# A mixture-of-experts layer on one Trainium2 core: one-hot rows shared out among three engines, gates interleaved in PSUM, and the gathered sum moved to VectorE

## The reference

```python
q = (h @ wq).reshape(B, S, PEER_HEADS, 2, PEER_QDIM // 2)
sub_scores = jnp.einsum('bshpk,hpnk->bshpn', q, subkeys)
top_v, top_i = lax.top_k(sub_scores, PEER_TOPK)
cand = top_v[..., 0, :, None] + top_v[..., 1, None, :]
cand_i = top_i[..., 0, :, None] * N_KEYS + top_i[..., 1, None, :]
best_v, best_pos = lax.top_k(cand.reshape(..., 256), PEER_TOPK)
expert = jnp.take_along_axis(cand_i.reshape(..., 256), best_pos, axis=-1)
gates = jax.nn.softmax(best_v, axis=-1)
hid = gelu(jnp.einsum('tkd,td->tk', u[expert], x), approximate=False) * gates
out = jnp.einsum('tk,tkd->td', hid, v[expert])
```

## Time and profile before

| what | value |
|---|---|
| median of 3 runs | 3908.99 us (3905.73 to 3910.11) |
| profiled execution | 3904.9 us |
| its span, first to last instruction | 3903.1 us |
| mean granted PE clock | 0.921 of full speed |
| busy, share of the span | PE 89%, PEld 72%, DVE 56%, ACT 37%, POOL 21% |
| gates, about 594 to 1012 us; dense, about 1012 to 1942 us | 418 us and 930 us |

### The profile page before, as it was taken

The page is one execution under the profiler, slowest core; times in us unless marked ns, Lnnn a source line. Parts: engine busy times, 40 slices in busy tenths (PEclk is TensorE's granted clock), DMA queues, the critical chain, the costliest instruction groups (busy, mean ns, idle before and its releaser), DMA issues.

```text
span 3903.1 us, 40841 instructions
## 1 busy us (share of the span) xinstructions
PE 3473.6 (89%) x16313; PEld 2806.0 (72%) x16313; DVE 2200.8 (56%) x3309; ACT 1446.3 (37%) x2342; POOL 830.0 (21%) x654
## 2 busy tenths in 40 slices
PE   5897998887799999999999997899898899899998
PEld 3466577777688888888878885678776574477887
DVE  2445597776588888888855524545532332344332
ACT  1222124665455555555532224444441111223222
POOL 0000102776355555555400000000000000000000
PEclk9895998989999999999989998899997598799999
DMA  4330522444888888888545522121121032022222
GB/s 170 130 114 1 195 75 102 168 161 147 303 302 293 306 298 294 305 298 293 205 130 184 186 95 81 68 84 69 59 92 37 1 97 86 6 97 82 97 97 76
DMA packets 189678, 574.02 MB, mean 147 GB/s; under 512 B 16368, under 2 KB 80496, under 8 KB 171056
## 3 DMA queue, kind: packets, MB, share of 16 engines
q1 hardware_dynamic: 152160, 369.80, 27.5%
q0 software_dynamic: 37328, 201.61, 14.3%
HBM read 523.69 MB, written 47.64 MB: 146 GB/s over the span
## 4 chain that ended last, share of the span: by engine, by line
PE 54%; DVE 32%; ACT 9%; issue 3%; DMA 2%; POOL 0%; SPq 0%; DVEq 0%; ACTq 0%; POOLq 0%
PE ps L228 10%; PE ps L230 10%; PE ps L229 10%; DVE peer_TG L1486 5%; PE ps L237 5%; DVE Wl L220 4%; DVE peerv_UV L1477 4%; DVE peerv_VL L1362 4%; DVE peerv_HI L1486 3%; ACT Wh L214 3%; PE ps L312 2%; PE ps L168 1%; ACT peerv_VH L1358 1%; ACT peerg_GB L1281 1%; DVE peerg_OH L1227 1%
## 5 line engine op out<-in xcount | busy, mean ns | idle before, releaser
L220 DVE TENSOR_TENSOR Wl<-W,Wh 128x1024 fp32r<-128x1024 f32 x363 | 438.7, 1209 | 778.8 <-ACT Wh L214 778.7
L214 ACT ACTIVATE Wh<-W 128x1024 fp32r<-128x1024 f32 x363 | 377.1, 1039 | 590.6 <-PE ps L230 569.5
L1409 POOL TENSOR_TENSOR peer_Y<-peer_Y,peerv_UV 128x1024 f32<-128x1024 f32 x128 | 392.8, 3069 | 383.2 <-ACT peerv_UV L1455 383.2
L1432 PE MATMUL ps<-peerv_VH,peer_HTh 128*128 128x512 f32 x768 | 304.1, 396 | 80.6 <-DVE peer_HTl L1489 80.6
L1191 PE MATMUL ps<-peer_Hh,Wh 128*128 128x384 f32 x1024 | 352.4, 344 | 15.7 <-DVE Wl L220 15.4
L1192 PE MATMUL ps<-peer_Hl,Wh 128*128 128x384 f32 x1024 | 347.4, 339 | 0.0
L1193 PE MATMUL ps<-peer_Hh,Wl 128*128 128x384 f32 x1024 | 347.2, 339 | 0.0
L1434 PE MATMUL ps<-peerv_VH,peer_HTl 128*128 128x512 f32 x768 | 301.5, 393 | 0.0
L1433 PE MATMUL ps<-peerv_VL,peer_HTh 128*128 128x512 f32 x768 | 301.1, 392 | 0.0
L228 PE MATMUL ps<-f_Hh,Wh 128*128 128x512 f32 x672 | 262.3, 390 | 2.2 <-DVE Wl L220 2.2
L230 PE MATMUL ps<-f_Hh,Wl 128*128 128x512 f32 x672 | 261.5, 389 | 0.0
(11 more groups left out here) (468 smaller groups left out, 7036.7 us busy)
## 6 DMA issues: line engine op xcount, KB each, us to landing
W<-peer_u SPq DMA_DIRECT2D x128, 512.0 KB, 6.6
peerv_VR<-peer_v SPq DMA_DIRECT2D x128, 512.0 KB, 5.5
gates_dram<-peerg_GB SPq DMA_DIRECT2D x12, 2048.0 KB, 7.4
peerv_GR<-gates_dram SPq DMA_DIRECT2D x32, 768.0 KB, 8.4
f_AW<-w_ada POOLq DMA_DIRECT2D x48, 512.0 KB, 4.1
W<-w_gate SPq DMA_DIRECT2D x44, 512.0 KB, 3.2
W<-w_up SPq DMA_DIRECT2D x44, 512.0 KB, 3.2
swa_AW<-w_ada POOLq DMA_DIRECT2D x32, 512.0 KB, 5.0
```

The lines of the kernel that those rows point to most:

```text
L214: A.then_inc(e.activation(w_parts(i)[0], w_raw(i), ACT.Copy), ("w_hi", i))
L220: V.then_inc(e.tensor_tensor(lo, w_raw(i), hi.bitcast(F32), SUB), ("w", i))
L1409: G.then_inc(e.tensor_tensor(Y, Y, UV[:, k % NUV, 1024:2048], ADD), ("y", k))
L1432: e.matmul(o, HTh[:, s, sl], VH[:, s, d], start=n == 0, stop=False)
```

## The change

It has four parts.

- Dense: ACT's scaling (L1455) and POOL's addition (L1409) go. DVE does both in one instruction, `Y = UV * HG + Y`, between `v_lo` of round j and the dot product of round j. POOL's stream in this stage is gathers alone, and each waits for DVE's sum 5 picks before.
- Gates, one-hot tiles: `OA` is made with its gate at once, four instructions a group with two scalar operands, on POOL where q % 3 is 1 and on DVE otherwise. `OB` is made by POOL where q % 3 is 0, in four instructions, and by ACT otherwise: four activations |JT - iota|, then, after waiting for them, one activation max(0, 1 - x) over the 512 columns. NOH goes from 5 to 6, and NHS from 3 to 2.
- Gates, layout: the matmul of token s writes every fourth column of the bank from s on, so that ACT's copy reads the bank straight and writes runs of 4 elements, where it wrote single elements 32 apart.
- Order: the last three copies of banks come before the last five "h" and not after them; and the split of the first tile of `u` moves from the start of gates into the query loop. The clearing of `Y` moves from POOL to DVE.

```diff
-    NOH, NHS = 5, 3
+    NOH, NHS = 6, 2
@@
-        + [("h", p) for p in range(FIRST + NQ // 3, NPRE)]
+        + [("q", NQ + i) for i in range(3)] + [("h", p) for p in range(FIRST + NQ // 3, NPRE)]
@@ query_act, and the same with w_lo in query_dve
-            if nb < 14:
-                w_hi(e, t_q[nb + 2])
+            if nb < 15:
+                w_hi(e, (t_q + t_u)[nb + 2])
@@
+    def oa_on_pool(q):
+        return q % 3 == 1
+    def ob_on_pool(q):
+        return q % 3 == 0
+    def oa(e, q):
+        for s in range(4):
+            c = 4 * q + s
+            ins = e.tensor_scalar(oh(q)[0][:, s, :], iota, IT[:, c:c + 1], GT[:, c:c + 1], EQ, MUL)
+        return ins
+    def gate_bank(q):
+        return ps(q % 5).rearrange("p (j s) -> p j s", s=4)
@@ gates_dve
-            oh_free(e, n)
-            V.then_inc(e.tensor_tensor(oh(n)[0], bc4(iota), keys_of(IT, n), EQ), ("oe", n))
-            if n % 2:
-                V.then_inc(e.tensor_tensor(oh(n)[1], bc4(iota), keys_of(JT, n), EQ), ("ob", n))
+            if not oa_on_pool(n) and n < NQ:
+                oh_free(e, n)
+                V.then_inc(oa(e, n), ("oa", n))
@@ gates_pool
-            if q % 2:
-                V.wait_ge(e, ("oe", q))
-                G.then_inc(e.tensor_tensor(OA, OA, keys_of(GT, q), MUL), ("oa", q))
-            else:
+            if oa_on_pool(q):
+                oh_free(e, q)
+                G.then_inc(oa(e, q), ("oa", q))
+            if ob_on_pool(q):
                 oh_free(e, q)
@@ gates_act
-            if n % 2 == 0 and n < NQ:
-                V.wait_ge(e, ("oe", n))
+            if not ob_on_pool(n) and n < NQ:
+                oh_free(e, n)
                 for s in range(4):
                     c = 4 * n + s
-                    ins = e.activation(oh(n)[0][:, s, :], oh(n)[0][:, s, :], ACT.Copy, scale=GT[:, c:c + 1])
-                A.then_inc(ins, ("oa", n))
+                    ins = e.activation(oh(n)[1][:, s, :], iota, ACT.Abs, scale=-1.0, bias=JT[:, c:c + 1])
+                A.then_inc(ins, ("ob1", n))
+                A.wait_ge(e, ("ob1", n))
+                ob = OH[:, n % NOH, 512:1024]
+                A.then_inc(e.activation(ob, ob, ACT.Relu, scale=-1.0, bias=1.0), ("ob", n))
@@
-                A.then_inc(e.activation(GB[h % 2][:, :, t:t + 4].rearrange("p j t -> p t j"), v4(ps(p % 5)), ACT.Copy),
-                           ("gb", p))
+                A.then_inc(e.activation(GB[h % 2][:, :, t:t + 4], gate_bank(p), ACT.Copy), ("gb", p))
@@ gates_pe
-                ins = e.matmul(ps(n % 5)[:, s * 128:s * 128 + 128], OA[:, s, :], OB[:, s, :], start=True, stop=True)
+                ins = e.matmul(gate_bank(n)[:, :, s], OA[:, s, :], OB[:, s, :], start=True, stop=True)
@@ dense_pool
-        for k in range(NUV):
+        for k in range(128):
             uv_load(e, k)
-        for k in range(128):
-            A.wait_ge(e, ("gv_", k))
-            G.wait_ge(e, ("y", k - 1))
-            G.then_inc(e.tensor_tensor(Y, Y, UV[:, k % NUV, 1024:2048], ADD), ("y", k))
-            uv_load(e, k + NUV)
@@ dense_act
-                A.wait_ge(e, ("hg", k))
-                v = UV[:, k % NUV, 1024:2048]
-                A.then_inc(e.activation(v, v, ACT.Copy, scale=HG[:, k:k + 1]), ("gv_", k))
@@ dense_dve
+        def y_add(k):
+            A.wait_ge(e, ("hg", k))
+            V.wait_ge(e, ("y", k - 1))
+            V.then_inc(e.scalar_tensor_tensor(out=Y, in0=UV[:, k % NUV, 1024:2048], scalar=HG[:, k:k + 1], in1=Y,
+                                              op0=MUL, op1=ADD), ("y", k))
@@
             v_lo(e, j)
+            if j:
+                y_add(j - 1)
             uv_in[j % NUV].wait_ge(e, ("uv", j))
```

More of the change, by code:

```diff
@@ L1072, in query_dve @@
         for nb in range(17):
-            if nb < 14:
-                w_lo(e, t_q[nb + 2])
+            if nb < 15:
+                w_lo(e, (t_q + t_u)[nb + 2])
             if nb:
@@ L1181, in oh_free @@
         V.wait_ge(e, ("chosen", q // 32))
-    def keys_of(x, q):
-        return x[:, 4 * q:4 * q + 4].unsqueeze(2).broadcast_to([128, 4, 128])
+    def oa_on_pool(q):
[7 more added lines that the diff above has]
+        return ins
     def hidden_pe(e, o, i, *keys):
@@ L1210, in pre_store @@
         hs_out[p % NHS].then_inc(e.dma_start(HID[p], HS[:, p % NHS, :]), ("hs", p))
+    def gate_bank(q):
+        return ps(q % 5).rearrange("p (j s) -> p j s", s=4)
     def gates_dve(e):
         behind(e, "query")
-        w_lo(e, t_u[0])
         ahead = best_dve(e, 0)
@@ L1223, in gates_dve @@
                 continue
-            if n % 32 == 0:
+            if n % 32 == 0 and n < NQ:
                 ahead = best_dve(e, n // 32 + 1)
-            oh_free(e, n)
-            V.then_inc(e.tensor_tensor(oh(n)[0], bc4(iota), keys_of(IT, n), EQ), ("oe", n))
-            if n % 2:
-                V.then_inc(e.tensor_tensor(oh(n)[1], bc4(iota), keys_of(JT, n), EQ), ("ob", n))
+            if not oa_on_pool(n) and n < NQ:
+                oh_free(e, n)
+                V.then_inc(oa(e, n), ("oa", n))
             if n % 2:
@@ L1236, in gates_pool @@
         behind(e, "query")
-        G.then_inc(e.memset(Y, 0.0), ("y", -1))
         for q in range(NQ):
-            OA, OB = oh(q)
-            if q % 2:
-                V.wait_ge(e, ("oe", q))
-                G.then_inc(e.tensor_tensor(OA, OA, keys_of(GT, q), MUL), ("oa", q))
-            else:
+            if oa_on_pool(q):
+                oh_free(e, q)
+                G.then_inc(oa(e, q), ("oa", q))
+            if ob_on_pool(q):
                 oh_free(e, q)
@@ L1246, in gates_pool @@
                     c = 4 * q + s
-                    ins = e.tensor_scalar(OB[:, s, :], iota, JT[:, c:c + 1], None, EQ)
+                    ins = e.tensor_scalar(oh(q)[1][:, s, :], iota, JT[:, c:c + 1], None, EQ)
                 G.then_inc(ins, ("ob", q))
     def gates_act(e):
-        w_hi(e, t_u[0])
         behind(e, "query")
@@ L1261, in gates_act @@
         run(ahead)
-        for kind, n in BESIDE + [("q", NQ + i) for i in range(3)]:
+        for kind, n in BESIDE:
             if kind == "h":
@@ L1299, in gates_pe @@
                 continue
+            if n >= NQ:
+                continue
             if n % 32 == 0:
                 picks = best_pe(e, n // 32 + 1)
-            (G if n % 2 else A).wait_ge(e, ("oa", n))
-            (V if n % 2 else G).wait_ge(e, ("ob", n))
+            (G if oa_on_pool(n) else V).wait_ge(e, ("oa", n))
+            (G if ob_on_pool(n) else A).wait_ge(e, ("ob", n))
             if n >= 5:
@@ L1319, in gates_sp @@
             w_load(e, i)
-        for kind, n in [("h", p) for p in range(FIRST)] + BESIDE + [("q", NQ + i) for i in range(3)]:
+        for kind, n in [("h", p) for p in range(FIRST)] + BESIDE:
             if kind == "h":
@@ L1395, in uv_load @@
             if k >= NUV:
-                G.wait_ge(e, ("y", k - NUV))
+                V.wait_ge(e, ("y", k - NUV))
             uv_in[k % NUV].then_inc(e.indirect_dma_start(
@@ L1468, in dense_dve @@
     def dense_dve(e):
+        def y_add(k):
[3 more added lines that the diff above has]
+                                              op0=MUL, op1=ADD), ("y", k))
         A.wait_ge(e, "hk")
+        V.then_inc(e.memset(Y, 0.0), ("y", -1))
         for j in range(128):
@@ L1489, in dense_dve @@
             V.then_inc(e.tensor_tensor(HTl[:, j % 2, :], x, HTh[:, j % 2, :].bitcast(F32), SUB), ("htl", j))
+        y_add(127)
     def sums(blk):
```

## The result

The changed kernel takes 3747.73 us (median; 3743.41 to 3751.27), against 3908.98 us before: a ratio of 0.9588, 95% interval 0.9572 to 0.9605, or 161 us. The forecast was 111 us, 3798 us, and the range ended at 3755. The profiled execution took 3751.3 us, its span is 3749.5 us, 153.6 less than before. The other 7 us of the 161 are scatter of single executions: the profiled one before was 4 us under its median, this one is 4 above.

What follows compares the result with a forecast made beforehand. Dense was bound by DVE waiting for POOL's addition, gates by ACT and DVE handing work back and forth. Gains 60 (dense) + 40 (gates) + 10 + 1 (edges) = 111 us gave 3798 us, range 3755 to 3855.

Steps and rivals of the forecast that it cites:

- What holds dense: Dense: DVE's product with the gates waits about 2.19 us a round for POOL's SBUF-reading addition; falls from 2.74 to 0.55.
- slow-product rival: Dense: the product with the gates is slow by itself, for its runs of 32 elements; 4004 us, chance 0.01.
- What is late next in dense: Dense: PE limits next, 6.75 us a round instead of 7.22, DVE's round 6.17; gain 60 us.
- PE never waits: Dense: bound with PE never waiting and the drains counted, 6.67 us a round, gain 70 us.
- The gathers: Dense: POOL's gathers, 972 ns each, collide with DVE at no cost; if they held DVE fully, gain 9 us.
- ACT and the copy in gates: Gates: copy falls from 1082 to 583 ns; ACT is 229 us busy, 7.2 us a unit, as full as PE.
- The strided matmul: Gates: writing every fourth column costs the same as packed; rival, a fraction of the rate, 4035 us, chance 0.04.
- The gates unit: Gates: a unit goes from 9.75 to 8.5 us, the middle above the floor 7.2; gain 40 us, from 0 to 72.
- The clock in gates: Gates: granted clock 0.91 left as it is, PE's time 7.1 us a unit.
- The lock at 9.0 us a unit: Gates: POOL's 4.8 and DVE's 4.2 us always exclude each other; in the rival that gates gives nothing, 3838 us, chance 0.20.
- The edges: Between gates and dense: earlier Gelu and stores gain 8 to 12 us, taken as 10; last Gelu to first gather about 6.
- The 1 us at the start of gates: Start of gates: first hidden round moves into PE's 15.1 us wait for a split; net gain 1 us.

Runs made afterwards that it cites:

- the two kernels with POOL work: Changed kernel with two SBUF-reading additions, or three write-only clearings, on POOL behind each gather of dense: 3863.4 us and 3742.1 us, one run each.
- the shares undone: Changed kernel with one-hot rows made as before (OA compared on DVE, scaled on ACT or POOL; OB on POOL or DVE): 3810.0 us, ratio 0.9752.
- the layout undone: Changed kernel with packed gate matmul outputs and ACT's copy writing single elements apart again: 3769.5 us, ratio 0.9648.

## Why the forecast was wrong, step by step

- **What holds dense.** Right. The product fell by 2.19 us to 0.55, with the new dense stage alone too, and the two kernels with POOL work show that it is POOL's reads and no other POOL work. The slow-product rival is excluded.
- **What is late next in dense.** Right in kind, PE; the term was mis-sized. The round is (1777.6 - 932.0) / 127 = 6.66 us. I had 6.67 as the bound "PE never waits" and added 0.08 for what two buffers can't smooth. There was nothing to add: PE is busy in all of 1000 to 1700 us. Dense gained 74.6 us for 60: 0.09 x 128 = 12 of the 15 us are here, and the other 3 are the round of the kernel before, 7.24 us between its dot products on average and not 7.22. DVE's round was mis-sized too, about 6.35 for 6.17, without effect, as it stays under PE's.
- **The gathers.** I costed their collision at nothing for DVE, and that held, though they grew from 0.97 to 1.68 us. Here POOL waits, and it has the time.
- **ACT and the copy in gates.** Right: the copy takes 583 ns as forecast, and four Abs rows and four scaling rows take the same, 1.27 and 1.28 us. ACT is busy 211 us where I had 229, mostly because a group of `OB` takes 1.85 us and not 2.1: next to nothing is lost between its two steps.
- **The strided matmul.** The packed value held, 275 ns at the median for one record in both layouts and 1.95 us for two groups. The Trainium skill's rule ("Advanced Engine Details and Errata", PSUM Cachelines) that such a pattern slows matmuls significantly does not show for a float32 matmul of 128 columns written 16 bytes apart. The rival falls.
- **The gates unit. This is the step that failed.** "I take the middle, 8.5" between a floor of 7.2 and the 9.75 of before: it came out at 237.6 / 32 = 7.42, from 309.7 / 32 = 9.68. That is 72 us for 40, three quarters of what the stretches gained beyond the forecast. The middle had no mechanism: it stood for waits that did not come. PE waits 14.5 us in the whole stretch, so nothing that was left (lock, splits, buffers) kept it far from its own pace; with the shares undone it is 9.4 us again.
- **The clock in gates** was the second slip of that step. I wrote "The granted clock is 0.91 here and I leave it so", but took PE's 7.1 from rows at a granted clock of 1.00 (rows 6, and 1.00 in 940 to 963 us around rows 8). PE was in fact busy 246.5 / 32 = 7.70 us a unit, and is 6.97 now, at 0.99. By the two clocks 246.5 us become 246.5 x 0.91 / 0.99 = 227, so some 20 of the 23 us that PE's busy time lost are the clock, an estimate. The clock follows PE's idle time in four runs: 63 us idle and 0.91 before, 59 and 0.93 with the shares undone, 24 and 0.99 with the layout undone, 15 and 0.99 in the changed kernel. No run moves one without the other.
- **The lock at 9.0 us a unit** did not bind. POOL's two instructions averaged 1066 and 763 ns with medians of 836 and 598, while DVE's scaling stayed at 342 with 517 at most, so where the two collide it is POOL that waits, and less work on POOL gains nothing.
- **The edges.** 8.9 us for 10; from the last Gelu of gates (918.03) to the first gather (921.85) it is now 3.8 us where I had about 6. The wait with two buffers of `HS` that I priced at nothing exists: ACT waits 14.8 us, six times, each wait ending within 11 us of the issue of a 2 MB store, and it costs PE next to nothing. The 1 us at the start of gates did not come: PE still waits 13.3 us there for the split, 15.4 before.

The two large terms failed in the same direction: each stood above the bound that PE's own time sets, while both stages ran at or near it. The range ended too high for a reason in its own sums. Its 72 us for gates is a unit of 7.5, but the floor that the prediction names is 7.2, and 32 x (9.75 - 7.2) = 82 us would have taken the range down to about 3745. Its 70 for dense was passed as well, by 5 us.

## What to carry to other kernels

When a wait that crosses engines is removed and the next bound is an engine that then has no gaps, take that engine's own time as the forecast, not a middle between it and the present, and let the range reach to it. Where the granted clock of a stretch is below 1 and the change closes PE's gaps, work out PE's time at both clocks: here the two moved together, and the clock was worth some 20 us of 72, by the estimate above. Two-input DVE work beside POOL instructions that read SBUF is the first thing to look for when one DVE instruction is several times as long as its form.

## What the runs showed of the hardware that I had not expected

- One record of a float32 matmul of 128 columns takes 275 ns whether its output is packed or every fourth column, and two groups of four matmuls take 1.95 us either way (before and after).
- ACT's copy of 512 elements from PSUM takes 1082 to 1090 ns with single float32 written 128 bytes apart, and 583 with runs of four.
- A gather's issue on POOL takes 0.94 to 1.06 us for the first five of the changed kernel, with no dot product beside them, and 1.68 us under one. That it waits for the end of that instruction is what the times suggest: the dot product's successor starts at 1307.04, and the gather ends 0.9 us later. No run isolates it.
